# Position bias of a streaming hybrid encoder: a Toeplitz matrix read from a periodic table in memory, where a Hankel matrix was read and reversed on TensorE

## The reference, cut to what matters

```python
dist = jnp.arange(CHUNK)[:, None] - r[None, :] + ATT_WINDOW
bias = table[:, jnp.clip(dist, -REL_CLIP, REL_CLIP) + REL_CLIP].astype(jnp.float32)
s = jnp.where(valid[None, :, None, None, :], s + bias[None, None], -jnp.inf)
p = jax.nn.softmax(s, axis=-1).astype(v.dtype)
```

## Time and profile before

| | us |
|---|---|
| median of 3 runs (903.09 to 903.89) | 903.75 |
| the profiled execution, its own time | 903.63 |
| span that the profile covers | 901.8 |

### The profile page before, as it was taken

One profiled execution on the slowest core, in us unless ns is written; L12 is line 12 of the kernel. 1 busy time (PEld: TensorE's weight loads), 2 busy tenths in 40 slices (PEclk: granted clock), 3 DMA queues, 4 the chain that ended last, 5 costly groups with the idle time before them and its releaser, 6 DMA issues.

```text
span 901.8 us, 17007 instructions
## 1 busy us (share of the span) xinstructions
PE 875.2 (97%) x6908; PEld 856.7 (95%) x6908; DVE 473.2 (52%) x755; ACT 311.2 (35%) x454; POOL 64.4 (7%) x51
## 2 busy tenths in 40 slices
PE   6999999999999999999995999999999999999997
PEld 6999999999999999899995899999999999999995
DVE  6332666665787677766338544334433443334336
ACT  6211545544523222455324332123312331133322
POOL 1000000000000000200435200000000000000223
PEclk9999999999999999999997999999999999999997
DMA  9222212321312121122221122222222222222202
GB/s 296 94 94 93 85 54 77 104 71 58 120 50 97 52 99 47 53 95 93 94 93 47 48 77 71 86 94 94 94 93 93 88 69 76 94 94 93 94 2 99
DMA packets 78450, 77.18 MB, mean 86 GB/s; under 512 B 2944, under 2 KB 76304, under 8 KB 78416
## 3 DMA queue, kind: packets, MB, share of 16 engines
q1 hardware_dynamic: 69328, 70.53, 23.9%
q10 hardware_dynamic: 8448, 4.02, 1.6%
q0 software_dynamic: 640, 2.17, 0.7%
HBM read 71.70 MB, written 4.99 MB: 85 GB/s over the span
## 4 chain that ended last, share of the span: by engine, by line
PE 93%; DVE 4%; issue 1%; POOL 1%; ACT 1%; DMA 0%; ACTq 0%; DVEq 0%
PE acc L746 76%; PE wk L770 3%; PE wk L746 3%; PE wk L884 3%; DVE scaled L1394 1%; DVE act_lo L1414 1%; PE wk L846 1%; PE wk L845 1%; POOL act_lo L414 1%; PE wk L803 1%; PE wk L954 1%; PE acc L770 1%; PE wk L962 1%; PE wk L794 1%; PE wk L952 0%
## 5 line engine op out<-in xcount | busy, mean ns | idle before, releaser
L474 ACT ACTIVATE w_hi<-w_raw 128x1024 fp32r<-128x1024 f32 x123 | 130.4, 1060 | 454.0 <-PE acc L746 441.6
L746 PE MATMUL acc<-act_hi,w_hi 128*128 128x272 f32 x1264 | 267.3, 293 | 13.1 <-DVE act_lo L1414 9.9
L746 PE MATMUL acc<-act_hi,w_lo 128*128 128x272 f32 x1264 | 262.7, 289 | 0.0
L746 PE MATMUL acc<-act_lo,w_hi 128*128 128x272 f32 x1264 | 262.0, 289 | 0.0
L746 PEld LDWEIGHTS acc<-act_hi,w_hi 128*128 128x128 f32 x1264 | 199.3, 189 | 18.8 <-DVE act_lo L1414 11.3
L746 PEld LDWEIGHTS acc<-act_lo,w_hi 128*128 128x128 f32 x1264 | 199.7, 190 | 0.0
L746 PEld LDWEIGHTS acc<-act_hi,w_lo 128*128 128x128 f32 x1264 | 198.7, 190 | 0.0
L1097 DVE TENSOR_TENSOR w_lo<-w_raw,w_hi 128x1024 fp32r<-128x1024 f32 x123 | 150.4, 1223 | 36.4 <-ACT w_hi L474 36.2
L746 PE MATMUL acc<-mid_hi,w_hi 128*128 128x272 f32 x608 | 125.4, 287 | 0.0
L746 PE MATMUL acc<-mid_hi,w_lo 128*128 128x272 f32 x608 | 125.0, 288 | 0.0
L746 PE MATMUL acc<-mid_lo,w_hi 128*128 128x272 f32 x608 | 124.8, 287 | 0.0
(11 more groups left out here) (205 smaller groups left out, 803.4 us busy)
## 6 DMA issues: line engine op xcount, KB each, us to landing
w_raw<-in_w_in SPq DMA_DIRECT2D x44, 512.0 KB, 4.4
w_raw<-in_w_ff_up SPq DMA_DIRECT2D x32, 512.0 KB, 4.3
w_raw<-in_w_ff_down SPq DMA_DIRECT2D x32, 512.0 KB, 4.1
w_raw<-in_w_o SPq DMA_DIRECT2D x8, 512.0 KB, 3.9
x_nat<-in_x_prompt SPq DMA_DIRECT2D x4, 512.0 KB, 5.2
w_raw<-in_w_attn_out SPq DMA_DIRECT2D x4, 512.0 KB, 3.7
w_raw<-in_w_ret_out SPq DMA_DIRECT2D x4, 512.0 KB, 4.7
k_cache<-in_cache_attn_k SPq DMA_DIRECT2D x1, 1024.0 KB, 11.9
```

Of the source, the lines that this page charges most:

```text
L474: act.activation(w_hi[:, v % 2], w_raw[:, v // 2, :, P * (v % 2):P * (v % 2) + P], ACT.Copy).then_inc(hi_ready, 1)
L746: ins = pe.matmul(dst[:, n, 0:HALF], w[:, k, :], h[:, k, HALF * n:HALF * n + HALF], start=begin, stop=end)
```

## The change

The table is handed over reversed. POOL puts it at the end of `table_row` and fills the beginning with the first value. The store to memory now writes each of the 8 rows 128 times, one behind the other, so that `table_ext` is 8 x 128 x 384 values. The load back steps by 383 values from partition to partition, one short of the period of 384, so each partition sees the row moved by one the other way: a Toeplitz matrix, which goes straight into `bias`. `flip`, its load, the 16 matmuls on PE and `bias_mm` are gone. DVE's subtraction reads SBUF only (with a small copy of the far value, `bias_far`, ahead of it), waits for the load, and stands before the last of the first three groups, which is taken out of the loop for that.

```diff
-            pool.dma_start(table_row[:, 0:TABLE], a["rel_bias_table"]).then_inc(table_in, 16)
+            far = 3 * P - TABLE
+            pool.dma_start(table_row[:, far:3 * P], a["rel_bias_reversed"]).then_inc(table_in, 16)
 
             pool.wait_ge(table_in, 16)
-            pool.tensor_copy(table_row[:, TABLE:3 * P],
-                             table_row[:, TABLE - 1:TABLE].to_broadcast([AH, 3 * P - TABLE])).then_inc(table_filled, 1)
+            pool.tensor_copy(table_row[:, 0:far], table_row[:, far:far + 1].to_broadcast([AH, far])).then_inc(table_filled, 1)
             pool.wait_ge(table_filled, 1)
-            pool.dma_start(table_ext, table_row[:]).then_inc(table_out, 16)
+            pool.dma_start(table_ext, table_row[:].unsqueeze(1).to_broadcast([AH, P, 3 * P])).then_inc(table_out, 16)
 
             pool.wait_ge(table_out, 16)
-            pool.dma_start(hankel[:], bass.AP(table_ext.tensor, 1, [[1, P], [3 * P, AH], [1, 2 * P]])).then_inc(hankel_in, 16)
+            pool.dma_start(bias[:], bass.AP(table_ext.tensor, far, [[3 * P - 1, P], [3 * P * P, AH], [1, 2 * P]])).then_inc(bias_in, 16)
...
-            act.dma_start(flip[:], a["flip"]).then_inc(const_in, 16)
...
-            pe.wait_ge(hankel_in, 16)
-            pe.wait_ge(const_in, 32)
-
+            pe.wait_ge(const_in, 16)
             pe.wait_ge(kc_ready, 1)
-            for h in range(AH):
-                for b in range(2):
-                    ins = pe.matmul(wk[:, 256 * h + P * b:256 * h + P * b + P], hankel[:, h, P * (1 - b):P * (1 - b) + P], flip[:],
-                                    start=True, stop=True)
-            ins.then_inc(bias_mm, 1)
...
-            with dve.Fori(0, G_RET) as g:
+            with dve.Fori(0, G_RET - 1) as g:
                 for j in range(4):
                     to_z(g, j, 4 * g + j)
                     split_ahead(g, j)
 
-            dve.wait_ge(bias_mm, 1)
-            order.after(dve.tensor_tensor(bias[:], wk[:].rearrange("p (h c) -> p h c", h=AH),
-                                          hankel[:, :, 2 * P - 1:2 * P].to_broadcast([P, AH, 2 * P]), ALU.subtract))
+            dve.wait_ge(bias_in, 16)
+            order.after(dve.tensor_copy(bias_far[:].unsqueeze(2), bias[:, :, 0:1]))
+            order.after(dve.tensor_tensor(bias[:], bias[:], bias_far[:].unsqueeze(2).to_broadcast([P, AH, 2 * P]), ALU.subtract))
 
             dve.memset(bias[0:AD, :, P + AD:2 * P], NEG).then_inc(bias_ready, 1)
+            for j in range(4):
+                to_z(G_RET - 1, j, 4 * (G_RET - 1) + j)
+                split_ahead(G_RET - 1, j)
```

More of the change, by code:

```diff
@@ L61, in shape_constants @@
     ident = np.eye(P, dtype=f)
-    flip = np.ascontiguousarray(ident[::-1])
     half = RD // 2
@@ L85, in shape_constants @@
         decay[:, h, P + 4] = np.exp(DEC * lg)
-    return {"ident": ident, "flip": flip, "ones": np.ones((P, P), f), "rope": rope, "decay": decay}
+    return {"ident": ident, "ones": np.ones((P, P), f), "rope": rope, "decay": decay}
 class Order:
@@ L176, in build @@
         x_nat = place("x_nat", [P, 5, D], at=z_at)
-        hankel = place("hankel", [P, AH, 2 * P], at=z_at + 4 * T * Z_RQ)
-        k_cache = place("k_cache", [P, 4, AH * AD], at=ends["hankel"])
+        k_cache = place("k_cache", [P, 4, AH * AD], at=z_at + 4 * T * Z_RQ)
         table_row = place("table_row", [AH, 3 * P], at=ends["k_cache"])
-        flip = place("flip_sb", [P, P], at=ends["table_row"])
-        x_waste = place("x_waste", [P, 2, D], at=ends["flip_sb"])
-        assert ends["x_nat"] <= z_at + 4 * T * Z_SPARE and ends["x_waste"] <= work_at
+        x_waste = place("x_waste", [P, 2, D], at=ends["table_row"])
+        bias_far = place("bias_far", [P, AH], at=ends["x_waste"])
+        assert ends["x_nat"] <= z_at + 4 * T * Z_SPARE and ends["bias_far"] <= work_at
         bias = place("bias", [P, AH, 2 * P], at=z_at + 4 * T * Z_SPARE)
@@ L236, in build @@
         wk_halves = [wk[:, 1024 * i:1024 * i + 1024].rearrange("p (n c) -> p n c", n=2) for i in range(2)]
-        table_ext = nc.dram_tensor("table_ext", (AH, 3 * P), fp, kind="Internal").ap()
+        table_ext = nc.dram_tensor("table_ext", (AH, P, 3 * P), fp, kind="Internal").ap()
         ident_in, const_in = sem("ident_in"), sem("const_in")
@@ L243, in build @@
         w_first, w_in_sem = sem("w_first"), [sem("w_loaded0"), sem("w_loaded1")]
-        cache_k_in, table_in, table_filled, table_out, hankel_in = (
-            sem("cache_k_in"), sem("table_in"), sem("table_filled"), sem("table_out"), sem("hankel_in"))
+        cache_k_in, table_in, table_filled, table_out, bias_in = (
+            sem("cache_k_in"), sem("table_in"), sem("table_filled"), sem("table_out"), sem("bias_in"))
         gains_in, x_tr, x_copied_act, x_copied_dve = sem("gains_in"), sem("x_tr"), sem("x_copied_act"), sem("x_copied_dve")
         x_hi, x_lo, x_sum_act, var_clear = sem("x_hi"), sem("x_lo"), sem("x_sum_act"), sem("var_clear")
-        kc_tr, kc_ready, bias_mm, bias_ready = sem("kc_tr"), sem("kc_ready"), sem("bias_mm"), sem("bias_ready")
+        kc_tr, kc_ready, bias_ready = sem("kc_tr"), sem("kc_ready"), sem("bias_ready")
         sum_mm, var_ready, std_ready, tok_rstd_ready, spread_mm, rstd_ready = (
@@ L1517 @@
             a = a[0]
+        if name == "rel_bias_table":
+            name, a = "rel_bias_reversed", np.ascontiguousarray(a[:, ::-1])
         arrays[name] = a
```

## The result

The changed kernel takes 921.1 us (median of 4 runs, 919.6 to 921.2), beside 903.4 for the kernel before (902.9 to 903.9): 1.0191 times, interval 1.0178 to 1.0204. It is slower by 17.7 us; the forecast was 918.8. The profiled execution has 921.04 us, 17.41 more than that of before.

The account below looks back on a forecast made before the run. PE, busy 97% of the span, was taken to bound the kernel: 903.63 - 3.6 (passes) + 17.0 (late tile 2) + 1.7 (clock) = 918.7 us profiled, 918.8 for the median; range 899.6 to 923 for 8 in 10.

Parts of the forecast that it names:

- the forecast's case: At the start, the store holds up SP's queue and PE by more than 10 us: 911 to 924 us, chance 0.59.
- PE's 32 passes, -3.6: Between groups 2 and 3, the reversal's 16 matmuls, two passes each, leave PE's stream: 3.6 us gained.
- DVE, 0: Before group 2, DVE's copy, subtraction and mask, 3.4 us at most, fit into 3.8 us idle: no cost.
- The store's pace: 1.57 MB out of 8 partitions: 7.9 us at the usual pace, 27.5 at 57 GB/s; the upper end taken.
- Turn by turn: On shared engines SP's queue gets one packet per store packet: 48 turns, leaving 74 of 122 packets, 3.7 us more.
- The second 128 columns: SP's load that ACT wants at 18.44 was to come late, at about 25, inside the same wait.
- the two weight loads that were to land after 40: Sign of being right: the weight loads issued at 9.9 and 10.8 land after 40 us.
- The second weight buffer: Before tile 2, it lands at 43.9 instead of 21.4, so PE starts tile 2 at 46.3, 17.0 us late.
- The clock: After PE's long wait, a lower granted clock costs 1.7 us, with 0 and 5 as bounds.
- (1): The store hides behind other work and only PE's 3.6 us count: 900.2 us (899.5 to 901), chance 0.30.
- rival 2: The store is slow, but less so: 901 to 911 us, the sum turning at a store of about 11.5 us; chance 0.09.
- (3): SP's packets pass, but the bias comes too late at DVE's wait: around 904 to 910 us, chance 0.02.

Follow-up runs that it names:

- the run with one copy: The changed kernel with the 8 table rows stored once (12 KB) and read into the bias with a step of one value: 899.9 us, 0.9954.
- Rows two and four apart: The changed kernel with its 8 table rows two or four partitions apart instead of in partitions 0 to 7: 906.1 us (1.0024) and 899.3 us (0.9947).
- the run of the store alone: The kernel before, reversal kept, with POOL also storing the 8 rows 128 times (1.57 MB) into a tensor nobody reads: 928.9 us, 1.0280.
- the two with half the copies: The changed kernel with 64 copies instead of 128, bias read in two loads: into 64 neighbouring partitions each, 913.2 us; into even, then odd partitions, 909.4 us.
- the one with the store later: The changed kernel with POOL issuing the store of the copies only when the second weight buffer has landed: 920.0 us, 1.0178.
- interleaved halves: The changed kernel with 64 copies instead of 128 and two bias loads, one into even and one into odd partitions: 909.4 us, 1.0070.

## Why the prediction was right

The result lies in the forecast's case, by its mechanism, in the order in which it was worked out:

- **PE's 32 passes, -3.6.** Right: 21.1 late behind group 1, 17.4 at the end; the run with one copy gives it alone (3.8 between medians).
- **DVE, 0.** Right: 2.29 + 0.17 + 0.48 in the gap, and the subtraction out of SBUF alone costs no more than with PSUM.
- **The store's pace**, the term that had to be bounded and in which I took the upper end: 27.5 us from the 32-row store's packets. It landed at 7.03 + 36.0 = 43.0; with the 0.6 for completion and packets from about 12.5 on, some 30 us, 53 GB/s instead of 57. Rows two and four apart show that the partitions set it, and that it counts where they lie: 8 partitions four apart went at the usual pace. So the step from 32 rows to 8, which goes by their number, came out because both stores read neighbouring partitions. Nothing in the earlier trace rows tells the two apart; this step had luck.
- **Turn by turn.** Right, 40 for 40. One can see in the same rows what the estimate assumed without a row: 8 engines. Two details were wrong without an effect on the sum. The second 128 columns, said to come at about 25, were on time (ACT rounds them at 17.89, at 18.44 before), so PE stood in two pieces and not in three. And of the two weight loads that were to land after 40, the profile gives the first as landed at 11.07 + 12.6 = 23.7; ACT waits for both.
- **The second weight buffer** landed at 46.7, not 43.9; with the 2.4 from there to PE, tile 2 at 49.1. So the 17.0 were 19.8, by the store's later begin (0.4) and slower pace (2.4).
- **The clock.** 1.3, taken as 1.7.

19.8 + 1.3 - 3.6 = 17.5, measured 17.41. The rivals: the store did not hide (1), was not fast enough (2), and the bias was there long before DVE came to it (3). One sum in rival 2 doesn't fit the rest: its break-even store of 11.5 us adds all of SP's packets behind the store, while the forecast lets 48 of the 122 pass beside it. By the forecast's way it is 30.5 - 12.1 - 3.7 - 0.6 = 14.1 us. Rows two apart, with 14.4 us from the store's first packet to its last, lost 4.5 us at tile 2 against a gain of 3.6, which is nearer to that. What the forecast didn't see is in the neighbourhood: it counted only the store as a hindrance, while the load behind it seems to be one too when it meets SP's queue before that has caught up, by my estimate some 3 us in the run of the store alone and the two with half the copies.

By the Trainium skill, SBUF — State Buffer, section on Door 1 (the DMA port swizzle), four neighbouring partitions share a port, partitions 0 to 7 reach two, rows two apart four and rows four apart eight, and a block of 64 partitions eight of the 16. The runs agree: the store goes at 53 GB/s over two, the packet's 722 ns become 320 and 180 with two and four times the ports, and the loads into 64 partitions side by side are slow where those into every second one aren't. An estimate from that section's 27.2 GB/s for a port is 54 GB/s over two.

By the Trainium skill, DMA: Bandwidth & Descriptors, section on why a DMA increments its semaphore by 16, the number of engines is the largest up to 16 that divides the slowest dimensions of both sides, which for this store's 8 and 1024 makes 8; the shares of 45.1% and 5.2%, 50% together, agree.

## What to carry to other kernels

A transfer whose few partitions lie side by side was slow in itself here (722 ns for a packet out of 8 neighbours, 180 out of 8 four apart), and it made another queue on its engines slow, one packet for one packet: price it by the time of its packets and by who loads beside it, not by its bytes. Spread its rows over the partitions (here four apart: 1.57 MB more in memory, no new wait on PE, 0.5% faster than before) rather than move it in time: this kernel streams weights, and in neither of the two places tried did 30 us of slow transfer go unnoticed. When a load is late, look for the buffer that is last at the engine, not for the wait that the profile names first.

## What was not expected of the hardware

- An issue by SP stood for 19.76 us in the changed kernel, 21.44 in the run of the store alone and 18.90 in the one with the store later, while half of the DMA engines had nothing to do. I read that as the full queue of the slow half stopping new work for the other half; no run looks into the queue.
- After tile 0 begins, PE's clock was at 1.2 GHz for some 3 us (0.52 from 15 to 18 us in the changed kernel; 6.8 us with interleaved halves) in six of the kernels, in three not (the one before among them), with no change there that I can name; tile 2 then begins 0.5 to 1 us later where nothing else is late. What decides it stays open.

```profile
15.00:18.00 3.00, 3.00 (x14) 3.00 (x15) 3.00 (x5) 3.00 (x6) 0.00 (x0) 0.52 0.85 166
```
